# An encoder layer with split fp32 products: where the high parts of eleven weight chunks are made

## The chip, the cores and the metric

The kernel runs on one core of a Trainium2 chip. The metric is the time on the device in microseconds (us), lower is better. All times of the trace are us from the start of the span of one profiled execution. The engines are TensorE (PE; PEld is its weight load), VectorE (DVE), ScalarE (ACT), GpSimd (POOL) and SyncE (SP). Each of SP, ACT and POOL can issue transfers; 16 DMA engines carry them all out.

## The reference

One encoder layer on 256 tokens of width 1024, followed by a final RMSNorm.

```python
h = rmsnorm(x, g1);  proj = h @ w_in + b_in          # q | k | v | lru-x | lru-gate | merge gates
attn = block_attention(rope(norm(q)), rope(norm(k)), v)
xc   = depthwise_conv(xr);  lru = rglru(xc, forward) + rglru(xc, backward)
rec  = lru * gelu(yr)
x    = x + (sigmoid(gA) * (attn @ w_attn_o) + sigmoid(gR) * (rec @ w_lru_o)) @ w_out
x    = x + moe_ffn(rmsnorm(x, g2))                   # 32 experts, top 4, clamped SwiGLU
out  = rmsnorm(x, final_g)
```

## The kernel before

**Two halves.** The first, to about 234 us, is the token mixer. It reads its weights as 15 chunks `pre[0..14]` of 128 rows by 4096 fp32 numbers, 2 MiB each (chunk 3 is half as wide). The second is the mixture of experts: 32 experts of 12 MiB each, in pieces of 2 MiB, stream through a ring of eight slots.

**Split products.** In the first half a product of fp32 operands is made of three passes over rounded operands (type fp32r): high by high, high by low, low by high (`product`, L1033). So every weight chunk `whole(c)` is turned into a high part `high(c)`, which is the chunk rounded to fp32r, and a low part `low(c) = whole(c) - high(c)`, which takes the place of the chunk itself. The high part lies in the slot beside the chunk. Three such pairs of slots turn in a ring, so chunk c can be loaded only when chunk c-3 has been used (`CONSUMED[c - 3]`, L245).

**Who makes the parts.** SP loads the whole chunk (L310). ACT rounds it to the high part in two instructions of 2048 columns (`split_high`, L386). For chunks 5 and 9 (`CAST_V`) DVE does it in one instruction (L631, recorded at L624). DVE subtracts (`split_low`, recorded at L627). PE waits for the low part (`chunk_in`, L1030), except for chunk 0: `first_groups` (L1065) starts with the high part and takes the low part as its last pass.

**What sets the order.** Each engine's program is written out by hand, and semaphores join them. At the start SP issues, without a wait: x in two loads, chunks 0 and 1, two rows of constants sent to all partitions, chunk 2, the tables and the first gate weights. ACT issues the unit squares `sq` and the small constants `cst` (L363, L364). DVE waits for `cst` at L619, works out the norm of x (L594, L600), and turns PE's transposes into `hT_hi` (two halves, L609 and L624) and `hT_lo`. PE's first product, L1078, waits for both ACT instructions on chunk 0 (`split_hi` 2) and for the first half of `hT_hi`. Later places named below: the gates of the recurrence (PE L1092, read by ACT at L419, the second set after the sum L767 on DVE), the rotary part on DVE (L713 to L734) and its transposes on PE (L1120), and the entry of the branches on PE at L1190, which waits for `rec_split` (DVE) and for `group_read` 32 (ACT L406). GpSimd does nothing but four constant fills.

Of the kernel before, what the change touches and what calls it, by code (L numbers as in the profile page):

```python
# [40 lines left out]
PAIRS = 3  # L41
PRE = 15
# [13 lines left out]
def encoder_layer(nc, x, consts, squares, rows, pre, w_lru, w_gu, w_down, b_down, out):  # L56
# [5 lines left out]
    with ctx:  # L62
# [3 lines left out]
        def sem(name):  # L66
            return ctx.enter_context(nc.semaphore(name))
# [113 lines left out]
        extra_full = [sem(f"extra_full{i}") for i in range(2)]  # L181
        lruw_in = sem("lru_weights_in")
        split_hi, split_lo = sem("chunk_high"), sem("chunk_low")
        h_hi, h_lo, rec_split, attn_split = (sem(n) for n in ("h_high", "h_low", "rec_split", "attn_split"))
        chunk_used = [sem(f"chunk_used{j}") for j in range(PER)]
        gu_done, dn_done = chunk_used[3], chunk_used[5]
# [29 lines left out]
        block = ctx.enter_context(nc.Block())  # L216
# [24 lines left out]
        def slot(s):  # L241
# [3 lines left out]
        CONSUMED = ([(group_done, 4), (group_done, 8), (qkv_done, T), (qkv_done, 2 * T)]  # L245
                    + [(group_done, 12 + 4 * i) for i in range(6)])

        IN_CHUNK, Q_CHUNK, BR_CHUNK, MIX_CHUNK = [0, 1, 4, 5, 6, 7, 8, 9], 2, [10, 11, 13], [12, 14]
        CAST_V = (5, 9)

        def casts_before(c):
            return 2 * sum(b not in CAST_V for b in range(c))

        WIDTH = [KD * 2 * KVW if c == Q_CHUNK + 1 else CH for c in range(PRE)]

# [2 lines left out]
        def low(c):  # L258
            return ring_r[PLACE[c]][:, 0:WIDTH[c]]

        def high(c):
            return (late_r if PLACE[c] == LOWS else ring_r[PLACE[c] + 1])[:, 0:WIDTH[c]]

        def whole(c):
            return ring[PLACE[c]][:, 0:WIDTH[c]]

        def landed(c):
            return slot_full[PLACE[c]], 16 * PLACE[:c + 1].count(PLACE[c])
# [93 lines left out]
        def _(act):  # L362
# [15 lines left out]
            def split_high(c, parts=range(2)):  # L378

                act.wait_ge(*landed(c))  # L380
                if c == 13:
                    act.wait_ge(lru_unit, 3)
                    act.wait_ge(pv_ps, NQ)
                w = WIDTH[c] // 2
                for i in parts:
                    nc.scalar.activation(high(c)[:, i * w:(i + 1) * w], whole(c)[:, i * w:(i + 1) * w],  # L386
                                         ACT.Copy).then_inc(split_hi, 1)
# [69 lines left out]
                sum_squares(hn, x_sb, t)  # L457
            root(1, slice(0, T))
            split_high(0)
            split_high(1)  # L460

            act.wait_ge(lam_e, 1)
            nc.scalar.activation(lam_t[1], lam_t[0], ACT.Exp, scale=-1.0).then_inc(lam_e, 1)
            for i in range(4):
                group(i)
            split_high(Q_CHUNK)
            for i in range(4, 8):
                group(i)
                if i == 5:
                    split_high(Q_CHUNK + 1)  # L470
            split_high(4)
            lru_gates(0, range(4))
            act.wait_ge(qk_inv, 1)
            nc.scalar.activation(qk_rstd, qk_rstd, ACT.Sqrt).then_inc(qk_rs, 1)
            split_high(6)
            for i in range(8, 14):
                group(i)
                if i % 2 == 1:
# [5 lines left out]
            act.wait_ge(group_read, 16)  # L484
            gelu_all = gelu[:, :, :].rearrange("p k n -> p (k n)")
            nc.scalar.activation(gelu_all, gelu_all, ACT.Gelu_apprx_tanh).then_inc(gelu_ok, 1)
            split_high(7)
            for i in range(16, 32):
                if 17 <= i < 21:
                    lru_gates(1, [i - 17])  # L490
                s = i - 18
                if 0 <= s - 2 < NQ:
                    h = s - 2
                    act.wait_ge(pT_ps, h + 1)
                    nc.scalar.activation(probT[:, h % 2, :, :].rearrange("p a n -> p (a n)"), ps[:, 2, :],
                                         ACT.Copy).then_inc(pT_ok, 1)
                if 0 <= s < NQ:
                    act.wait_ge(max_ok, s + 1)
                    for t in range(T):
                        b = (s % 2) * T + t  # L500
                        nc.scalar.activation(prob[:, s % 2, t, :], ps[:, s % 2, t * TOK:(t + 1) * TOK], ACT.Exp,
                                             bias=neg_max[:, b:b + 1], scale=HD ** -0.5,
                                             accum_out=exp_sum[:, b:b + 1]).then_inc(exp_ok, 1)
                if i % 2 == 1:
                    group(i - 1)
                    group(i)
                if 20 <= i < 23:
                    lru_decay(1, i - 20)
                if i == 24:
                    lru_root(1)  # L510
                if i in (18, 19):
                    split_high(8, [i - 18])
                if i in (26, 27):
                    split_high(10, [i - 26])
                if i == 30:
                    split_high(11)
            load_sqrt_table(2)
            for c in range(12, PRE):
                split_high(c)
# [55 lines left out]
            for t in range(T):  # L575
# [3 lines left out]
                                     accum_out=ssum[:, t:t + 1]).then_inc(sq_sum, 1)  # L579
                root(4 + t, slice(t, t + 1))  # L580

        @block.vector
        def _(dve):
            steps = [0]

            def link(ins):

                steps[0] += 1
                ins.then_inc(v_step, 1)
                dve.wait_ge(v_step, steps[0])  # L590
# [32 lines left out]
            def high_part(dst, whole):  # L623
                return nc.vector.tensor_copy(dst, whole)  # L624

            def low_part(dst, whole, hi):
                return nc.vector.tensor_tensor(dst, whole, hi.bitcast(f32), ALU.subtract)  # L627

            def split_high(c):
                dve.wait_ge(*landed(c))  # L630
                link(high_part(high(c), whole(c)))  # L631

            def split_low(c):

                if c not in CAST_V:
                    dve.wait_ge(split_hi, casts_before(c) + 2)
                low_part(low(c), whole(c), high(c)).then_inc(split_lo, 1)

            lam = cst[:, C_LAM:C_LAM + 16]
# [28 lines left out]
            for c in range(KD):  # L668
# [4 lines left out]
                b = cst[:, C_CB + c:C_CB + c + 1]  # L673
# [31 lines left out]
            link(nc.vector.tensor_reduce(qk_rstd, w1.rearrange("p (g d) -> p g d", d=HD), AX.X, ALU.add))  # L705
            link(nc.vector.tensor_scalar(qk_rstd, qk_rstd, 1.0 / HD, EPS, ALU.mult, ALU.add))
            nc.vector.reciprocal(qk_rstd, qk_rstd).then_inc(qk_inv, 1)
            split_high(5)
            split_low(5)
            dve.wait_ge(qk_rs, 1)  # L710
            for t in range(T):
# [100 lines left out]
            for s in range(NQ + 3):  # L812
                if 1 <= s <= NQ:
                    head_norm(s - 1)
                if s < NQ:
                    head_max(s)
                if s >= 4 and s % 2 == 0:
                    pair_attn((s - 4) // 2)

                if s == 0:  # L820
                    split_low(7)
                if s == 2:
                    split_low(8)
                if s == 3:
                    lru_input(1)
                if s == 5:
                    lru_square(1)
                if s == 6:
                    split_high(9)
                    split_low(9)  # L830
                if s == 7:
                    lru_scaled(1)
                if s == 8:
                    lru_scan(1)
                    split_low(10)
                if s == 9:
                    lru_sum(1)
                    recurrent_branch()
                if s == 10:
                    recurrent_split()  # L840
# [647 lines left out]
```

## Time and profile before

| | us |
|---|---|
| median of three runs | 1166.57 |
| the three runs | 1162.07, 1167.43, 1166.57 |
| span of the profiled execution | 1161.2 |
| PE busy | 1081.6 |
| ACT busy | 234.2 |
| DVE busy | 382.9 |
| GpSimd busy | 0.2 |

Of the profiled execution the span is what is given; the median of the runs, which are timed from outside, is 5.4 us above it and the lowest 0.9 us. Read the first half and the second apart: in the first PE is busy nearly without a gap and the DMA engines have room, in the second the DMA engines are full and PE waits in small pieces.

### The profile page before, as it was taken

The numbers are of one execution on the slowest core, as the hardware profiler recorded it, in microseconds if no ns is written. First come the engines' busy times: TensorE is split into PE (matmuls) and PEld (weight loads), VectorE is DVE, ScalarE is ACT, GpSimd is POOL, SyncE is SP. The second block draws the span as 40 slices with busy tenths as digits, with TensorE's granted clock in tenths as the row PEclk, the third lists the DMA queues.
The fourth block names the chain that finished last, engine by engine and source line by source line (L and its number), as shares of the span: only waits on it lengthen the run. The fifth ranks groups of instructions, "written<-read, shape, count | busy, mean of one in ns | idle before, by whom it ended". The sixth has DMA issues, their size and how long they took to land.

```text
span 1161.2 us, 13145 instructions
## 1 busy us (share of the span) xinstructions
PE 1081.6 (93%) x5391; PEld 502.8 (43%) x5391; DVE 382.9 (33%) x671; ACT 234.2 (20%) x371; POOL 0.2 (0%) x4
## 2 busy tenths in 40 slices
PE   5998999989999999999998989898989898989997
PEld 5998789823333333333333323332333233323332
DVE  6996798532322222222121212121211212121122
ACT  5388843100111111111111111111110101010112
POOL 0000000000000000000000000000000000000000
PEclk9999999989999999999999999999999999999999
DMA  8543146998999999999999999999999999999996
GB/s 351 186 171 145 73 160 278 418 400 333 429 397 425 431 425 429 428 428 429 428 429 428 430 428 427 430 428 428 430 428 428 429 428 430 428 427 429 429 428 248
DMA packets 32618, 439.89 MB, mean 379 GB/s; under 512 B 3760, under 2 KB 3888, under 8 KB 5712
## 3 DMA queue, kind: packets, MB, share of 16 engines
q1 hardware_dynamic: 32112, 438.53, 89.9%
q10 hardware_dynamic: 480, 0.99, 0.2%
q8 instruction: 19, 0.31, 0.1%
q14 instruction: 7, 0.06, 0.0%
HBM read 438.46 MB, written 1.05 MB: 378 GB/s over the span
## 4 chain that ended last, share of the span: by engine, by line
PE 61%; DMA 33%; DVE 4%; ACT 1%; issue 1%; SPq 0%; DVEq 0%
DMA slot<-in_w_gu_dram 27%; PE ps L1333 25%; PE ps L1037 12%; PE ps L1342 10%; DMA slot<-in_w_down_dram 6%; PE ps L1305 4%; PE ps L1286 3%; PE ps L1300 1%; PE ps L1387 1%; DVE slot_r L627 1%; PE ps L1092 1%; PE ps L1135 1%; PE ps L1264 1%; PE ps L1156 1%; PE ps L1365 0%
## 5 line engine op out<-in xcount | busy, mean ns | idle before, releaser
L1333 PE MATMUL ps<-slot,lru 128*64 128x512 f32 x880 | 198.9, 595 | 21.0 <-DMA slot<-in_w_gu_dram 20.7
L1342 PE MATMUL ps<-slot,lru 128*64 128x512 f32 x896 | 203.3, 596 | 14.8 <-DMA slot<-in_w_down_dram 14.3
L1333 PE MATMUL ps<-slot,qT 128*64 128x512 f32 x880 | 202.1, 601 | 14.4 <-DMA slot<-in_w_gu_dram 12.9
L1333 PEld LDWEIGHTS ps<-slot,lru 128*64 128x64 f32 x880 | 62.7, 137 | 147.6 <-issue 113.5
L1333 PEld LDWEIGHTS ps<-slot,qT 128*64 128x64 f32 x880 | 62.5, 137 | 147.1 <-issue 134.9
L1342 PEld LDWEIGHTS ps<-slot,lru 128*64 128x64 f32 x896 | 62.3, 137 | 135.4 <-issue 117.1
L558 ACT ACTIVATE lru<-ps 128x512 f32<-128x512 f32 x32 | 19.1, 598 | 419.7 <-PE ps L1333 419.7
L993 DVE TENSOR_TENSOR lru<-ps,cst 128x1024 f32<-128x1024 f32 x32 | 39.2, 1225 | 141.5 <-PE ps L1387 141.5
L970 DVE TENSOR_SCALAR lru<-sq,x_sb,small 128x64 f32<-128x64 f32 x66 | 17.7, 312 | 188.1 <-PE ps L1286 188.1
L1037 PE MATMUL ps<-wide_r,slot_r 128*128 128x256 f32 x492 | 66.2, 286 | 0.2 <-DVE slot_r L627 0.2
L1305 PE MATMUL ps<-lru 128*128 128x512 f32 x136 | 63.9, 593 | 0.9 <-DVE lru L1017 0.9
L1286 PE MATMUL ps<-hn,lru 128*64 128x512 f32 x264 | 63.7, 600 | 0.9 <-DVE lru L907 0.9
L987 DVE COPY lru<-ps 128x512 f32<-128x512 f32 x32 | 22.1, 692 | 127.6 <-PE ps L1333 127.6
L1037 PEld LDWEIGHTS ps<-wide_r,slot_r 128*128 128x128 f32 x492 | 61.3, 191 | 4.6 <-issue 4.1
L560 ACT ACTIVATE lru<-lru 128x512 f32<-128x512 f32 x32 | 20.2, 632 | 198.3 <-DVE lru L997 198.3
L627 DVE TENSOR_TENSOR slot_r<-slot,slot_r 128x4096 fp32r<-128x4096 f32 (+1 forms) x14 | 59.7, 4268 | 0.3 <-ACT slot_r L386 0.2
L544 ACT ACTIVATE qT<-ps 128x512 f32<-128x512 f32 x33 | 19.7, 598 | 160.7 <-PE ps L1286 160.7
L937 DVE TENSOR_TENSOR qT<-ps,cst 128x512 f32<-128x512 f32 x16 | 11.1, 692 | 116.6 <-PE ps L1300 116.6
L386 ACT ACTIVATE slot_r<-slot 128x2048 fp32r<-128x2048 f32 (+1 forms) x24 | 43.1, 1838 | 22.1 <-DMA slot<-in_pre_dram 22.1
L551 ACT ACTIVATE lru<-ps 64x512 f32<-64x512 f32 x63 | 37.3, 592 | 39.4 <-PE ps L1342 38.7
L1387 PEld LDWEIGHTS ps<-sq,lru 128*128 128x128 f32 x256 | 30.9, 193 | 26.8 <-issue 25.2
L937 DVE TENSOR_TENSOR lru<-ps,cst 128x512 f32<-128x512 f32 x17 | 11.8, 692 | 89.5 <-PE ps L1300 89.5
(212 smaller groups left out, 905.1 us busy)
## 6 DMA issues: line engine op xcount, KB each, us to landing
slot<-in_w_gu_dram SPq DMA_DIRECT2D x110, 2048.0 KB, 34.9
slot<-in_w_down_dram SPq DMA_DIRECT2D x55, 2048.0 KB, 33.2
wide<-in_w_gu_dram SPq DMA_DIRECT2D x15, 2048.0 KB, 34.8
slot<-in_pre_dram SPq DMA_DIRECT2D x14, 2048.0 KB, 8.3
wide<-in_w_down_dram SPq DMA_DIRECT2D x8, 2048.0 KB, 35.3
slot<-in_w_lru_dram SPq DMA_DIRECT2D x2, 1024.0 KB, 13.3
wide<-in_w_gu_dram SPq DMA_DIRECT2D x2, 1024.0 KB, 14.8
late<-in_w_gu_dram SPq DMA_DIRECT2D x1, 2048.0 KB, 16.8
```

The costliest lines, as they stand in the source:

```text
L386: nc.scalar.activation(high(c)[:, i * w:(i + 1) * w], whole(c)[:, i * w:(i + 1) * w], ACT.Copy).then_inc(split_hi, 1)
L551: nc.scalar.activation(pair_out[i // 2 % 2][rs, side * BANK:(side + 1) * BANK], ps[64 * side:64 * side + 64, bank, :], ACT.Copy).then_inc( ...
L627: return nc.vector.tensor_tensor(dst, whole, hi.bitcast(f32), ALU.subtract)
L937: nc.vector.tensor_tensor(xgT[i % 2].rearrange("p (h k) n -> p k h n", h=2), ps[:, 7, :].rearrange("p (k h n) -> p k h n", k=KD // 2, h=2) ...
L987: nc.vector.tensor_copy(gu_sb[:, 0:BANK], ps[:, 4, :]).then_inc(gu_v, 1)
L993: nc.vector.tensor_tensor(gub.rearrange("p (j n) -> p j n", j=16), ps[:, 4:6, :].rearrange("p b (j n) -> p (b j) n", n=CAP), bias.unsqueez ...
L1037: ins = nc.tensor.matmul(dst, st[a], mv[b], start=start and q == 0 and k == 0, stop=stop and q == 2 and k == len(sides) - 1)
L1286: ins = nc.tensor.matmul(ps[64 * h:64 * h + 64, 7, :], sel_next[:, t, :], x2[:, t, h * BANK:(h + 1) * BANK], start=(t == 0), stop=(t == T ...
L1305: return nc.tensor.matmul(ps[:, n, :], sgT[pair][:, n // 2, :], pair_out[pair][:, (n % 2) * BANK:(n % 2 + 1) * BANK], start=False, stop=last)
L1333: ins = nc.tensor.matmul(ps[64 * side:64 * side + 64, 4 + b, :], xgT[i % 2][:, k, :], rows[r][:, o:o + BANK], start=(k == 0), stop=(k == K ...
L1342: ins = nc.tensor.matmul(ps[64 * side:64 * side + 64, bank, :], actT[(i - 1) % 2][:, k, :], w[:, r, side * BANK:(side + 1) * BANK], start= ...
L1387: ins = nc.tensor.transpose(ps[:, 4 + j // 4, j % 4 * P:(j % 4 + 1) * P], gu_sb[:, j::KD], ident)
```

## The change

The high parts of chunks 1 to 11 are no longer made from the chunk in SBUF. GpSimd's queue issues a second load of the same rows of `pre`, whose destination is the fp32r tensor, so that the transfer rounds. ACT keeps the casts of chunks 0, 12, 13 and 14 (`CAST_A`). DVE's two casts go. Before its subtraction DVE now waits for both loads of the chunk (`landed`, `high_landed`) where it waited for ACT's cast. GpSimd's loads follow the same rule of release as SP's (`CONSUMED[c - PAIRS]`); those of chunks 1 and 2 wait for nothing.

```diff
-        CAST_V = (5, 9)
+        CAST_A = (0, 12, 13, 14)
...
+        def high_landed(c):
+            return high_in[c % PAIRS], 16 * sum(b % PAIRS == c % PAIRS for b in range(c + 1) if b not in CAST_A)
...
             split_high(0)
-            split_high(1)
...
+        @block.gpsimd
+        def _(pool):
+            for c in range(PRE):
+                if c in CAST_A:
+                    continue
+                if c >= PAIRS:
+                    pool.wait_ge(*CONSUMED[c - PAIRS])
+                pool.dma_start(high(c), pre[c, :, 0:WIDTH[c]]).then_inc(high_in[c % PAIRS], 16)
...
-            def split_high(c):
-                dve.wait_ge(*landed(c))
-                link(high_part(high(c), whole(c)))
-
             def split_low(c):
 
-                if c not in CAST_V:
+                if c in CAST_A:
                     dve.wait_ge(split_hi, casts_before(c) + 2)
+                else:
+                    dve.wait_ge(*landed(c))
+                    dve.wait_ge(*high_landed(c))
                 low_part(low(c), whole(c), high(c)).then_inc(split_lo, 1)
```

The calls `split_high(1)`, `(2)`, `(3)`, `(4)`, `(6)`, `(7)`, `(8)`, `(10)` and `(11)` on ACT and `split_high(5)` and `(9)` on DVE are taken out where they stood; nothing else moves.

GpSimd's program, which before the change ends with its constant fills:

```order
L1478 ISA
L1478 MEMSET const-float32-0.0 128x1
L1478 MEMSET const-float32-1.0 128x1
L1478 MEMSET const-bfloat16-1.0 128x1
L1478 MEMSET const-uint8-127 128x1
```

and the same with the change (`slot_r` are the high parts, `in_pre_dram` the chunks in memory):

```order
L1475 MEMSET const-uint8-127 128x1
L573 UNCONDITIONAL_BRANCH [waits barrier_Pool_Activation_PE_DVE_SP_gather]
L580 DMA slot_r<-in_pre_dram 128x4096 x2
L580 DMA slot_r<-in_pre_dram 128x2048 [waits group_done]
L580 DMA slot_r<-in_pre_dram 128x4096 [waits group_done]
L580 DMA slot_r<-in_pre_dram 128x4096 [waits qkv_done] x2
L580 DMA slot_r<-in_pre_dram 128x4096 [waits group_done] x5
```

Eleven loads have come in, the first two of them at the very start.

ScalarE's program from the root of the first norm on, before:

```order
L371 ACTIVATE small<-small 128x2 [waits var_inv]
L386 ACTIVATE slot_r<-slot 128x2048 [waits slot_full0]
L386 ACTIVATE slot_r<-slot 128x2048
L386 ACTIVATE slot_r<-slot 128x2048 [waits slot_full2]
L386 ACTIVATE slot_r<-slot 128x2048
L463 ACT_TABLE_LOAD
L463 ACTIVATE small<-small 128x16 [waits lam_exp]
L397 ACTIVATE xr_flat<-ps,cst 128x256 [waits half_bias_ok,margins,group_done]
L397 ACTIVATE xr_flat<-ps,cst 128x256 [waits group_done] x3
L386 ACTIVATE slot_r<-slot 128x2048 [waits slot_full4]
L386 ACTIVATE slot_r<-slot 128x2048
```

and now:

```order
L375 ACTIVATE small<-small 128x2 [waits var_inv]
L390 ACTIVATE slot_r<-slot 128x2048 [waits slot_full0]
L390 ACTIVATE slot_r<-slot 128x2048
L466 ACT_TABLE_LOAD
L466 ACTIVATE small<-small 128x16 [waits lam_exp]
L401 ACTIVATE xr_flat<-ps,cst 128x256 [waits half_bias_ok,margins,group_done]
L401 ACTIVATE xr_flat<-ps,cst 128x256 [waits group_done] x7
```

Chunk 0 (`slot_full0`) is still rounded here; chunks 1 and 2 are not.

VectorE's program at chunk 5, between the norm of q and k and the rotary part, before:

```order
L705 TENSOR_REDUCE small<-xr_flat 128x20 [waits v_step]
L706 TENSOR_SCALAR small<-small 128x20 [waits v_step]
L707 RECIPROCAL small<-small 128x20 [waits v_step]
L624 CAST slot_r<-slot 128x4096 [waits slot_full4]
L627 TENSOR_TENSOR slot_r<-slot,slot_r 128x4096 [waits v_step]
L713 TENSOR_TENSOR xr_flat<-late,small 128x640 [waits qk_rs]
```

and now:

```order
L704 TENSOR_REDUCE small<-xr_flat 128x20 [waits v_step]
L705 TENSOR_SCALAR small<-small 128x20 [waits v_step]
L706 RECIPROCAL small<-small 128x20 [waits v_step]
L627 TENSOR_TENSOR slot_r<-slot,slot_r 128x4096 [waits chunk_high_in2,slot_full4]
L711 TENSOR_TENSOR xr_flat<-late,small 128x640 [waits qk_rs]
```

The cast is gone, and the subtraction waits for two loads, with the rotary part queued behind it.

## Rows read from the trace of the kernel before

**Rows 1.** The page: busy share of the DMA engines, 40 slices of 29 us.

```profile
DMA  8543146998999999999999999999999999999996
```

**Rows 2.** Stretches: start:end and length, busy us (x instructions) of PE, PEld, DVE, ACT, POOL, clock, DMA share, GB/s.

```profile
27.00:64.00 37.00, 36.27 (x228) 32.42 (x228) 35.21 (x69) 17.33 (x26) 0.00 (x0) 1.00 0.55 199
64.00:104.00 40.00, 36.84 (x294) 35.94 (x293) 32.98 (x35) 34.76 (x50) 0.00 (x0) 1.00 0.36 132
104.00:168.00 64.00, 62.88 (x425) 53.04 (x424) 52.26 (x66) 48.01 (x92) 0.00 (x0) 1.00 0.28 103
...
240.00:290.00 50.00, 47.34 (x197) 17.09 (x198) 10.98 (x34) 4.31 (x6) 0.00 (x0) 0.96 0.90 355
...
330.00:1161.00 831.00, 772.78 (x3504) 274.90 (x3500) 175.47 (x338) 91.36 (x153) 0.00 (x0) 1.00 0.99 421
```

**Rows 3.** Who waited for whom, 0 to 240 us: us in total, times, longest.

```profile
PE ps L1092 <- ACT lru L419: 3.6, 4, 3.2
...
PE ps L1037 <- DVE wide_r L627: 1.1, 1, 1.1
...
PE ps L1078 <- ACT slot_r L386: 0.7, 1, 0.7
...
PE ps L1037 <- DVE slot_r L627: 0.2, 1, 0.2
```

**Rows 4.** Timeline of the start: start, us, engine, line, operation [idle before it, releaser].

```profile
6.56 1.06 ACT L366 ACTIVATE hn<-x_sb 128x1024 f32<-128x1024 f32 x1 [3.38 <-DMA x_sb<-in_x_dram]
...
7.84 0.17 DVE L619 TENSOR_SCALAR cst<-cst 128x16 f32<-128x16 f32 x1 [6.88 <-DMA cst<-in_consts_dram]
...
11.52 3.71 ACT L386 ACTIVATE slot_r<-slot 128x2048 fp32r<-128x2048 f32 x2 [2.13 <-DMA slot<-in_pre_dram]
...
15.29 4.10 PE L1078 MATMUL ps<-wide_r,slot_r 128*128 128x256 f32 x32 [0.65 <-ACT slot_r L386]
15.61 0.69 DVE L624 CAST wide_r<-slot 128x1024 fp32r<-128x1024 f32 x1
...
18.55 8.76 DVE L627 TENSOR_TENSOR slot_r<-slot,slot_r 128x4096 fp32r<-128x4096 f32 x2
...
27.36 2.17 PE L1037 MATMUL ps<-wide_r,slot_r 128*128 128x256 f32 x16 [0.25 <-DVE slot_r L627]
```

**Rows 5.** Stretches of 2 us near the start, columns as in rows 2.

```profile
2.00:4.00 2.00, 0.00 (x0) 0.00 (x0) 0.00 (x0) 1.17 (x2) 0.00 (x0) 1.00 0.81 288
...
10.00:12.00 2.00, 1.02 (x5) 1.05 (x6) 0.84 (x2) 0.48 (x1) 0.00 (x0) 1.00 1.00 426
```

**Rows 6.** DMA issues by line: count, KB each, median us from issue to landing.

```profile
slot<-in_pre_dram SPq DMA_DIRECT2D x14, 2048.0 KB, 8.3
...
x_sb<-in_x_dram SPq DMA_DIRECT2D x2, 512.0 KB, 4.8
...
cst<-in_consts_dram ACTq DMA_DIRECT2D x1, 68.0 KB, 6.6
```

**Rows 7.** The page's groups: ACT's casts (busy, mean ns | idle before), and one of DVE's from the timeline.

```profile
L386 ACT ACTIVATE slot_r<-slot 128x2048 fp32r<-128x2048 f32 (+1 forms) x24 | 43.1, 1838 | 22.1 <-DMA slot<-in_pre_dram 22.1
...
63.64 2.23 DVE L624 CAST slot_r<-slot 128x4096 fp32r<-128x4096 f32 x1
```

**Rows 8.** Timeline, three later places of the first half.

```profile
79.25 0.50 DVE L734 COPY pbuf<-late 128x256 f32<-128x256 f32 x2
...
81.00 1.04 PE L1120 MATMUL ps<-sq,late 128*128 128x128 f32 x8
...
88.27 0.84 ACT L400 ACTIVATE late<-ps,cst 128x256 f32<-128x256 f32 x2 [0.85 <-PE ps L1037]
...
166.73 0.84 ACT L406 ACTIVATE xr_flat<-ps,cst 128x256 f32<-128x256 f32 x2 [1.31 <-PE ps L1037]
...
167.81 2.17 PE L1037 MATMUL ps<-lru_r,slot_r 128*128 128x256 f32 x16 [1.12 <-DVE wide_r L627]
```

**Rows 9.** SP's queue, 0 to 400 us: what the issue of the ring's loads waited for.

```profile
SPq L293 <- PE ps L1333: 113.5, 22, 17.9
```

More of the change, by code:

```diff
@@ L183, in encoder_layer @@
         split_hi, split_lo = sem("chunk_high"), sem("chunk_low")
+        high_in = [sem(f"chunk_high_in{i}") for i in range(PAIRS)]
         h_hi, h_lo, rec_split, attn_split = (sem(n) for n in ("h_high", "h_low", "rec_split", "attn_split"))
@@ L248, in encoder_layer @@
         IN_CHUNK, Q_CHUNK, BR_CHUNK, MIX_CHUNK = [0, 1, 4, 5, 6, 7, 8, 9], 2, [10, 11, 13], [12, 14]
-        CAST_V = (5, 9)
+        CAST_A = (0, 12, 13, 14)
         def casts_before(c):
-            return 2 * sum(b not in CAST_V for b in range(c))
+            return 2 * sum(b in CAST_A for b in range(c))
+        def high_landed(c):
+            return high_in[c % PAIRS], 16 * sum(b % PAIRS == c % PAIRS for b in range(c + 1) if b not in CAST_A)
         WIDTH = [KD * 2 * KVW if c == Q_CHUNK + 1 else CH for c in range(PRE)]
@@ L465, in _ @@
                 group(i)
-            split_high(Q_CHUNK)
             for i in range(4, 8):
                 group(i)
-                if i == 5:
-                    split_high(Q_CHUNK + 1)
-            split_high(4)
             lru_gates(0, range(4))
@@ L474, in _ @@
             nc.scalar.activation(qk_rstd, qk_rstd, ACT.Sqrt).then_inc(qk_rs, 1)
-            split_high(6)
             for i in range(8, 14):
@@ L486, in _ @@
             nc.scalar.activation(gelu_all, gelu_all, ACT.Gelu_apprx_tanh).then_inc(gelu_ok, 1)
-            split_high(7)
             for i in range(16, 32):
@@ L510, in _ @@
                     lru_root(1)
[L511 to L516, printed above, removed]
             load_sqrt_table(2)
@@ L707, in _ @@
             nc.vector.reciprocal(qk_rstd, qk_rstd).then_inc(qk_inv, 1)
-            split_high(5)
             split_low(5)
@@ L828, in _ @@
                 if s == 6:
-                    split_high(9)
                     split_low(9)
```

## The prediction, made before the result was known

> **What bounds the kernel now.** I read the busy tenths of the page first, then the stretches, then who waited for whom, then the timeline at the places that these name. The tenths show the DMA engines with room only between about 30 and 175 us [rows 1]. The stretches say why: from 27 to 168 us PE is busy 36.27 of 37, 36.84 of 40 and 62.88 of 64 us, all at a granted clock of 1.00 (the upper level, 2.4 GHz), while the DMA share is 0.55, 0.36 and 0.28 [rows 2]. After 330 us the DMA share is 0.99 at 421 GB/s [rows 2]: the experts are a stream of fixed bytes. SP's loads for the ring wait for PE to free slots [rows 9], and in 240 to 290 us the DMA share is still 0.90 [rows 2], so the stream can't start ahead of PE. Hence the rule of the whole sum: PE's first half sets when the stream runs, and a shift of PE in the first half, either way, arrives at the end one for one.
>
> So the question is what PE waits for in the first half. Between its first product and 240 us, waits that an engine of the casts ended are few [rows 3]: 0.65 us for ACT's cast of chunk 0, 0.25 us for DVE's low part of chunk 1, 1.12 us for the split of the recurrent branch, and 3.6 us for ACT's reads of the recurrence's gates. The rest is the start: PE's products begin at 15.29 us, released by ACT's cast of chunk 0, which ran from 11.52 to 15.23 right after that chunk had landed [rows 4].
>
> **What the change removes.** On ACT, 18 of the casts (26 in all, of which the group in [rows 7] holds 24), at a mean of 1.84 us [rows 7] about 33 us. On DVE two casts, near 2.23 us each [rows 7], 4.5 us. How much of that lies on the path?
> - Chunk 1's low part held PE for 0.25 us [rows 4]. It was DVE's own queue (two subtractions, 8.76 us in a row), not ACT. In the new kernel PE's start moves later than DVE's (below), and this wait goes: -0.25.
> - At 167.81 PE waited 1.12 us for DVE's split. DVE now comes 2.3 us earlier, having lost a cast at chunk 9. But PE also waits there for ACT's last read, which starts when PE's last group ends (at 166.7, row with 1.31 us idle) and ends at 167.57 [rows 8]. So 167.81 becomes about 167.67: -0.15.
> - The largest wait, 3.2 of the 3.6 us before the second set of gates [rows 3], comes down a chain that begins with ACT's read at 88.27, itself released by PE (0.85 us idle) [rows 8], then root, scans and sum. No cast of ACT or DVE lies in it: 0.
> - All other casts lie beside a busy PE. ACT's queue is shorter, which nobody waits for: 0.
> The gain is 0.4 us, and it can't be more than 0.65 + 0.25 + 1.12, about 2 us, even if every wait at a cast went.
>
> **What it adds.** Eleven loads, 10 x 2.10 + 1.05 = 22.0 MB, at 426 GB/s [rows 5] 52 us of all DMA engines. Nine of them, for chunks 3 to 11, start in stretches where the DMA share is 0.28 to 0.55 [rows 2], with PE two chunks away from needing them. The tightest is chunk 5, with both loads released as PE's third chunk is used and chunk 6's close behind: four transfers of 2.10 MB, 20 us at full rate, where one takes 8.3 us to land now [rows 6]. Behind DVE's wait for it stands the rotary part, which ends at 79.75 for a PE that comes at 81.00 [rows 8]: 1.25 us of slack and 2.23 us from the cast that is gone, 3.5 us. With the pairs sharing evenly chunk 5 lands near 63 us, about when DVE is there (63.64): 0.
>
> The two that wait for nothing, chunks 1 and 2 (4.19 MB), are another matter. Up to 11.5 us the DMA engines are what everybody waits for: from 4 us on they run full (426 GB/s at 10 to 12 us) [rows 5], and x, the small constants and chunk 0 are on the path. Whatever GpSimd's stream moves before chunk 0 has landed delays chunk 0 by its bytes / 426 GB/s. How many bytes is that? No row shows GpSimd's queue. The nearest row on sharing is ACT's: its 68 KB of constants took 6.6 us to land, longer than 512 KB of x (4.8) [rows 6], since their small packets took turns with SP's large ones. I take one packet of each queue in turn, and a packet to be a row of the transfer. Then on each DMA engine x is 16 packets of 4 KiB, chunk 0 is 8 of 16 KiB, and GpSimd's stream is 16 of 16 KiB. SP's first bytes move from 2 us on; by 4 us some 0.6 of the 1.4 MB of x, squares and constants are through (288 GB/s for 2 us) [rows 5], so about 9 packets of x are left. If GpSimd's stream is there by then, 9 + 8 = 17 turns come before chunk 0 is complete, and all 16 of GpSimd's packets go ahead of it: **4.19 MB / 426 GB/s = +9.8 us**. From below: a stream that starts after 11.5 us costs 0. From above: a rounding transfer that runs at half rate holds the engines for twice as long, +19.7 us. Between these ends I take 9.8, as GpSimd has nothing else to do at the start and SP's first issue shows that queues open at once.
>
> What is late next: x would land some 7 us later instead of at 6.5, so the norm, the transposes and both halves of `hT_hi` (the second ends at 16.30 now [rows 4]) come at about 23.5. Chunk 0 lands at 21.3 and its cast ends at 25.1: chunk 0 stays the later one, PE starts at 15.29 + 9.8 = 25.1. DVE's low part of chunk 0 then runs 25.1 to 29.5, that of chunk 1 to 33.9, while PE's first groups last 12 us, to 37: covered, chunk 1's 4.4 us and both loads of it too.
>
> From 2 to 4 us DVE is busy 0.00 us [rows 5], so nothing on it could hold back what GpSimd does at the start. The Trainium skill, SBUF — State Buffer, section "Who interferes with whom", has a rule by which it could: while VectorE runs a two-port copy or tensor_scalar, GpSimd can't write its descriptors and its DMA stands still. No row here can show that; with an idle VectorE the delay of chunk 0 stays 9.8 us by the rule as without it, and later it could only stretch loads that have cover.
>
> **Sum.** +9.8 - 0.25 - 0.15 = +9.4 us, made in the profiled execution: a span of 1161.2 + 9.4 = 1170.6. The 5.4 us between that span and the median lie outside both, so 1166.57 + 9.4 = **1176.0 us**, +0.8%.
>
> **Rivals.**
> - A, as summed, 8 to 11 us later at the start: 1174 to 1178. Chance 0.42.
> - B, a smaller share: GpSimd's packets are smaller than a row, say 4 KiB. 17 turns of 16 engines x 4 KiB are 1.1 MB, +2.6 us, less 0.4: 1168.8. A start of the stream only at 6 us, with x through and 8 turns left, gives 2.1 MB, +4.9 - 0.4: 1171.1. 
> - C, not slower: GpSimd's first descriptors come so late that chunk 0 has landed. The mechanism is the same sharing, and its point is 11.5 us: a stream whose first packet comes after that costs nothing, and 0.4 us are won, 1166.2. Against it: 11 us are long for a queue that has nothing ahead of it. Chance 0.13.
> - D, the rounding halves the rate of its transfers: +19.7 - 0.4, 1185.9, and chunk 5's high part, with 3.5 us of slack, may add 1 or 2. For it: rounding is work that a copy doesn't have; no row prices it. Chance 0.16.
> - E, something in the first half gains that I count as covered; bounded by the 2 us above, it would read as no change. Chance 0.05.
>
> **How the numbers follow.** The likeliest is A: 1176.0. The range takes in B, A and D and leaves C and E and the tail of D out: 1168 to 1187. A measurement of this kernel tells about 0.5% (5.8 us) from no change. Slower by more: A, D and the upper edge of B, 0.62. Within: most of B, C and E, 0.32. Faster by more: only what the scatter of the runs could give, 0.06.
>
> **What would show it.** In the profile after: ACT's first cast (chunk 0) near 21 instead of 11.5 us, and PE's first product near 25; x landing near 13; then the same PE stretches as before, shifted by the same amount, with no new wait of DVE for a load that reaches PE; ACT's busy time down 33 us with no wait of PE for ACT gone but at the start. It would be wrong if GpSimd's packets came after 11.5 us or were few before that (then C or B), if the first half became shorter than the shift by more than 2 us (then a cast was on the path that I don't see), or if DVE idled for loads at chunks 4 to 6 (D).

## The result, and the profile after

The changed kernel took 1174.14 us (median of 6 runs, 1168.97 to 1176.82) beside 1163.68 us (6 runs, 1162.07 to 1167.43) for the kernel before: a ratio of 1.008, 95% interval 1.0063 to 1.0097. It is slower, by some 9.3 us by the ratio and by 10.5 by the two medians; forecast were +9.4 us and 1176.0. The profiled execution has a span of 1171.7 us, 10.5 more than that of before.

That agreement is better than the reasoning was. The early stream cost less than I had summed, and in the profiled execution two things that I had not summed cost the rest. First the page: busy time by engine, the DMA tenths in 40 slices, the queues, and the two groups of DMA issues.

```profile
PE 1086.0 (93%) x5391; PEld 506.2 (43%) x5391; DVE 378.9 (32%) x669; ACT 203.7 (17%) x353; POOL 6.2 (1%) x15
...
DMA  9896557998999999999999999999999999999995
...
q0 software_dynamic: 1584, 22.02, 4.5%
...
slot<-in_pre_dram SPq DMA_DIRECT2D x14, 2048.0 KB, 11.4
slot_r<-in_pre_dram POOLq DMA_DIRECT2D x10, 2048.0 KB, 13.5
```

Queue 0 is GpSimd's: 22.02 MB, as counted from the diff. The hollow in the DMA tenths [rows 1] is partly filled. A load for chunk 1 to 14 takes 11.4 us to land in the median, where it took 8.3 [rows 6]. Now the start: timeline, start, us, engine, line, operation, and the idle time before it with its releaser. It answers to [rows 4].

```profile
1.23 1.19 POOL L580 DMA_DIRECT2D slot_r<-in_pre_dram  x2 [0.78 <-POOLq L1475]
...
7.99 1.06 ACT L370 ACTIVATE hn<-x_sb 128x1024 f32<-128x1024 f32 x1 [4.80 <-DMA x_sb<-in_x_dram]
...
10.49 0.17 DVE L619 TENSOR_SCALAR cst<-cst 128x16 f32<-128x16 f32 x1 [9.53 <-DMA cst<-in_consts_dram]
...
17.85 3.71 ACT L390 ACTIVATE slot_r<-slot 128x2048 fp32r<-128x2048 f32 x2 [6.59 <-DMA slot<-in_pre_dram]
...
21.61 5.54 PE L1075 MATMUL ps<-wide_r,slot_r 128*128 128x256 f32 x32 [5.12 <-ACT slot_r L390]
```

GpSimd issues its two loads at 1.23 us. Chunk 0 is there at 17.85 and not at 11.52 (+6.33), and PE's first product starts at 21.61 and not at 15.29 (+6.32). x is late by 1.4 us only. The first 32 products then take 5.54 us where they took 4.10. Who had the DMA engines? The queues in two stretches of 1 us, 4 to 5 and 5 to 6 (queue, kind: packets, MB, share of 16 engines; q1 is SP's, q10 ACT's):

```profile
q1 hardware_dynamic: 94, 0.33, 81.4%
q10 hardware_dynamic: 76, 0.08, 24.8%
...
q0 software_dynamic: 14, 0.23, 57.7%
q1 hardware_dynamic: 45, 0.18, 45.4%
q10 hardware_dynamic: 47, 0.03, 8.2%
```

and in 8 to 10 us, the window asked for as 8:10:

```profile
q1 hardware_dynamic: 27, 0.44, 53.2%
q0 software_dynamic: 26, 0.43, 50.8%
q10 hardware_dynamic: 26, 0.01, 1.7%
```

GpSimd's first packet moves only after 5 us, some 4 us after the issue: one packet of its queue from 5.0 to 5.2 us, seven from 5.2 to 5.4. From 8 to 10 us the three queues take turns packet by packet (27, 26, 26), and SP gets half of the bytes. If a stream that takes half starts at s, what SP had left to move until 11.5 us takes twice as long, so chunk 0 lands at s + 2 x (11.5 - s) = 23 - s. This is an estimate, made after the result. With s = 5.2, as read, it gives 17.8; measured 17.85. It isn't always so close: two kernels below, whose stream starts at 5.5 us (none of its packets before), should land chunk 0 at 17.5 and do at 18.13 and 18.30.

The next place is the hole before the second set of gates. Timeline of PE, of before and then of after:

```profile
101.75 1.97 PE L1092 MATMUL ps<-wide,slot 128*128 128x256 f32 x8 [3.16 <-ACT lru L419]
...
104.70 2.17 PE L1037 MATMUL ps<-wide_r,slot_r 128*128 128x256 f32 x16
...
107.67 0.60 PE L1092 MATMUL ps<-wide,slot 128*128 128x256 f32 x2
```

```profile
108.95 2.51 PE L1089 MATMUL ps<-wide,slot 128*128 128x256 f32 x8 [3.15 <-ACT lru L423]
...
113.39 3.78 PE L1034 MATMUL ps<-wide_r,slot_r 128*128 128x256 f32 x16
...
117.96 0.60 PE L1089 MATMUL ps<-wide,slot 128*128 128x256 f32 x2
```

The same products, 5.92 us before and 9.01 after, are 3.1 us longer, and the stretches show at which clock. Columns as in [rows 2], of after, an undisturbed stretch and this one:

```profile
27.00:64.00 37.00, 37.00 (x264) 34.97 (x263) 34.73 (x64) 3.68 (x9) 2.11 (x4) 1.00 0.85 330
...
110.00:120.00 10.00, 10.00 (x42) 7.90 (x41) 5.89 (x6) 5.09 (x13) 0.53 (x1) 0.66 0.11 23
```

From 27 to 64 us PE is busy all the time at 1.00, with the DMA share up from 0.55 to 0.85: the later loads don't reach it. From 110 to 120 us the granted clock is 0.66, between its upper level (2.4 GHz) and its lower (1.2), just behind a hole of 3.15 us in PE's work. The whole account of the profiled execution:

| PE reaches | before | after | later by |
|---|---|---|---|
| first product | 15.29 | 21.61 | 6.32 |
| second groups | 27.36 | 34.67 | 7.31 |
| transposes of the rotary part | 81.00 | 88.21 | 7.21 |
| second set of gates | 101.75 | 108.95 | 7.20 |
| the set after it | 107.67 | 117.96 | 10.29 |
| recurrent branch | 167.81 | 177.96 | 10.15 |
| first product of the experts | 240.34 | 250.45 | 10.11 |
| span | 1161.2 | 1171.7 | 10.5 |

6.3 us come from the start; 1.0 up to the second groups, where the first 32 products are 1.44 slower and 0.46 are won where the low part of chunk 1 was waited for, 0.25 of it the wait itself; 3.1 go with the lower clock, and -0.14 come at the branch. The 10.11 at the experts become 10.5 by the end. The waits of PE between 0 and 260 us, which answer to [rows 3], show only these two for engines of the casts and the gates:

```profile
PE ps L1075 <- ACT slot_r L390: 5.1, 1, 5.1
...
PE ps L1089 <- ACT lru L423: 3.6, 4, 3.2
```

Not all runs carry the same. The six runs of the changed kernel had mean granted clocks of 0.994, 0.994, 0.993, 0.991, 0.987 and 0.987, at 1168.97, 1169.42, 1173.29, 1175.0, 1176.82 and 1175.33 us. The two at 0.994 lie some 5.5 us over the median of before, near what the start alone costs. The clock doesn't order all runs, though: at 1173.29 it was 0.993.

### The profile page after: what moved, and what is told of

Its sections match the earlier page's. It is cut to its first block, busy times and chain, and to the rows that moved or that the text cites. A ratio compares the mean times of both kernels' runs of the same rounds, so it can differ in the third digit from the quotient of the medians.

```text
span 1171.7 us, 13145 instructions
## 1 busy us (share of the span) xinstructions
PE 1086.0 (93%) x5391; PEld 506.2 (43%) x5391; DVE 378.9 (32%) x669; ACT 203.7 (17%) x353; POOL 6.2 (1%) x15
## 3 DMA queue, kind: packets, MB, share of 16 engines
q0 software_dynamic: 1584, 22.02, 4.5%
## 4 chain that ended last, share of the span: by engine, by line
PE 63%; DMA 34%; DVE 1%; ACT 1%; issue 1%; SPq 0%; DVEq 0%
DMA slot<-in_w_gu_dram 27%; PE ps L1330 25%; PE ps L1034 13%; PE ps L1339 10%; DMA slot<-in_w_down_dram 6%; PE ps L1302 4%; PE ps L1283 3%; DMA slot<-in_pre_dram 1%; PE ps L1075 1%; PE ps L1297 1%; PE ps L1384 1%; PE ps L1089 1%; PE ps L1132 1%; PE ps L1153 1%; PE ps L1261 1%
## 5 line engine op out<-in xcount | busy, mean ns | idle before, releaser
L1384 PE MATMUL ps<-sq,lru 128*128 128x128 f32 x256 | 37.0, 287 | 0.8 <-DVE lru L984 0.8
## 6 DMA issues: line engine op xcount, KB each, us to landing
slot<-in_pre_dram SPq DMA_DIRECT2D x14, 2048.0 KB, 11.4
```

The costliest lines, as they stand in the source:

```text
L1384: ins = nc.tensor.transpose(ps[:, 4 + j // 4, j % 4 * P:(j % 4 + 1) * P], gu_sb[:, j::KD], ident)
```

## The experiments

My theory: packets of a second stream take turns with chunk 0's at the start, everything else in the change is covered, and the stretch of lower clock has a cause of its own. Rivals: the nine later loads or the removed casts matter (E), the rounding is what is expensive (D), the size of packets or the start of the stream decides (B).

**Casts of chunks 1 and 2 back on ScalarE.** The nine later loads stay; the two early ones go.

```
-        CAST_A = (0, 12, 13, 14)
+        CAST_A = (0, 1, 2, 12, 13, 14)
...
             split_high(0)
+            split_high(1)
...
                 group(i)
+            split_high(Q_CHUNK)
```

> The changed kernel, but with the high parts of chunks 1 and 2 made by ScalarE again, so that GpSimd's queue carries only chunks 3 to 11, each released as PE uses a chunk. Theory (the whole loss is the two loads that wait for nothing and go ahead of chunk 0): chunk 0 lands at 11.5 us and PE's first product starts at 15.3 as before, and the time is that of the kernel before to within 2 us, since the nine later loads and the casts that they replace are both hidden. Rival 1 (the later loads cost too, through DMA contention or VectorE's wait at chunk 5): PE's first product at 15.3, yet 3 us or more slower than before. Rival 2 (the casts taken away did cost something): faster than before by over 2 us.

Measured: 1164.38 us (12 runs) beside 1164.97 for before, ratio 1.0002 [0.9991, 1.0014]. The recurrent branch starts after 0.98 us of idle PE, where before had 1.12: the gain of 0.14 is there, and too small for the time to show. Nine loads of 18 MB in place of 14 casts on ScalarE and two on VectorE are together worth nothing here that the interval shows, in either direction; whether a small gain and a small cost cancel wasn't tried. Its profile has one more thing to keep in mind: chunk 0 is there at 11.71, the first product starts at 15.47 after 0.67 us of idle PE, all as before, and yet the first 32 products take 5.70 us and not 4.10.

**Only the two early loads, all other casts as before.**

```
+        BY_LOAD = (1, 2)
...
+        @block.gpsimd
+        def _(pool):
+            for c in BY_LOAD:
+                pool.dma_start(high(c), pre[c, :, 0:WIDTH[c]]).then_inc(high_in[c], 16)
...
```

> The kernel before, with only chunks 1 and 2 rounded by GpSimd's loads at the start; all other casts as before. Theory (early loads): the whole loss of the change: chunk 0 lands near 17.9 us instead of 11.5, PE's first product near 21.6 instead of 15.3, time 7 to 10 us above before. Rival (later loads carry the loss): under 3 us above before.

Measured: 1173.31 us (6 runs), ratio 1.0073 [1.0054, 1.0091]. So the two early loads account for the whole of the loss, within the intervals; with the run above, the early and the later loads have each been tried alone. Its profile shows both extra terms once more (chunk 0 at 18.13, first product at 21.89, 6.33 us for the first 32), and here the clock can be seen in the first products too. Stretches of 20 to 25, 25 to 30 and 110 to 120 us:

```profile
20.00:25.00 5.00, 3.11 (x14) 3.11 (x15) 3.92 (x2) 3.34 (x4) 0.00 (x0) 0.52 1.01 423
25.00:30.00 5.00, 5.00 (x37) 5.00 (x36) 5.00 (x2) 0.00 (x0) 0.00 (x0) 0.80 1.08 449
...
110.00:120.00 10.00, 9.98 (x35) 7.97 (x36) 4.16 (x3) 7.12 (x14) 0.00 (x0) 0.54 0.00 0
```

**Is it the rounding?** The kernel before, with its casts, and GpSimd copies the same 4.19 MB without rounding into a buffer that is idle then. Nobody reads the copies; ScalarE waits for them before it writes the gates there (left out of the cut above; so it is in the next two kernels with copies).

```
+        @block.gpsimd
+        def _(pool):
+            for i in range(2):
+                pool.dma_start(lru[:, i * CH:(i + 1) * CH], pre[1 + i, :, :]).then_inc(idle_in, 16)
```

> As the run with plain copies on ScalarE's queue, but issued by GpSimd. Theory (rounding costs the transfer nothing, the late start belongs to GpSimd's queue): first packets near 5 us, chunk 0 lands near 17.9 us, as with the rounding loads, x at 8.0. Rival (rounding is what starts late or runs at another rate): chunk 0 lands over 1 us away from 17.9, towards 21 if the plain stream starts early.

Measured: 1171.09 us (4 runs), ratio 1.0051 [1.0033, 1.0069]. Chunk 0 lands at 18.30, no earlier than with rounding (17.85; 18.13 in the run above, whose stream starts at 5.5 us as this one's does), and the first product starts at 22.06. The rounding costs a transfer nothing that shows: D falls. The queues of the changed kernel from 8 to 10 us say the same: 0.44 + 0.43 + 0.01 MB in 2 us are 440 GB/s, with the rounding stream as half of it.

**The same copies on ScalarE's queue,** behind the squares and the constants.

```
             act.dma_start(cst[:, 0:C_COS], consts[:, 0:C_COS]).then_inc(cst_in, 16)
+            for i in range(2):
+                act.dma_start(lru[:, i * CH:(i + 1) * CH], pre[1 + i, :, :]).then_inc(idle_in, 16)
```

> The kernel before with all its casts, and 4.19 MB more to load at the start: chunks 1 and 2 once more, as plain copies on ScalarE's queue into space that is idle until the recurrence's gates. If the delay of chunk 0 is the bytes that get in ahead of it in equal turns of the queues, and the 6.3 us of the change (not 9.8) come from GpSimd's stream starting only at 5 us, then here, with the stream there from 2.6 us on, x is held back by several us (first ScalarE instruction on it at 10 us or later instead of 6.6) and chunk 0 lands at 20 to 21.5 us instead of 11.5: 9 to 10 us later, time 9 to 13 us above before. Rival (a queue's share, not its start, made the 6.3): chunk 0 lands near 18 us here too.

Measured: 1169.81 us (5 runs), ratio 1.0042 [1.0026, 1.0058]; chunk 0 at 15.46, first product at 19.22. That missed what I expected (20 to 21.5, +9 to 13 us), and my rival's 18 too. I had taken the issue (1.67 us) for the start. But from 5 to 6 us ACT's queue still moves its small packets, 83 of them with 0.04 MB in all, and so it does until 7.5 us. ACT's queue from 7 to 7.5 and from 7.5 to 8 us, then both queues from 8 to 10 us:

```profile
q10 hardware_dynamic: 16, 0.00, 2.8%
...
q10 hardware_dynamic: 13, 0.15, 69.2%
...
q1 hardware_dynamic: 28, 0.46, 53.5%
q10 hardware_dynamic: 23, 0.38, 43.9%
```

ACT's queue works in order here, and one turn moves one packet, so the squares (256 KB) and the 68 KB of constants, in packets of about 0.5 KB at the end, hold up the 2 MB loads behind them for as long as they need turns. The stream begins at 7.5 us, and 23 - 7.5 is 15.5; measured 15.46. I formed the rule of 23 - s on this miss. It can't hold for a stream that has run out before chunk 0 is there; then all its bytes go ahead, which the next two try.

**A stream that is there at once:** the copies first on ScalarE's queue, the squares and the constants on GpSimd's.

```
-            act.dma_start(sq[:, :, :], squares).then_inc(sq_in, 16)
-            act.dma_start(cst[:, 0:C_COS], consts[:, 0:C_COS]).then_inc(cst_in, 16)
+            for i in range(2):
+                act.dma_start(lru[:, i * CH:(i + 1) * CH], pre[1 + i, :, :]).then_inc(idle_in, 16)
...
+            pool.dma_start(sq[:, :, :], squares).then_inc(sq_in, 16)
+            pool.dma_start(cst[:, 0:C_COS], consts[:, 0:C_COS]).then_inc(cst_in, 16)
```

> The kernel before with all its casts, and 4.19 MB more to load: plain copies of chunks 1 and 2 as the first thing on ScalarE's queue, with the squares and the small constants moved to GpSimd's. It tries the assumption of the prediction as it stood: a stream that is there from about 2.5 us on. Expected by it: x, in packets of 4 KiB that take turns with packets of 16 KiB, lands at 13 to 15 us instead of 6.6, chunk 0 at about 21.3 instead of 11.5, PE's first product near 25, the time 9 to 13 us above before. Rival (the delay never exceeds about 6.5 us): chunk 0 at 18.

Measured: 1174.27 us (4 runs), ratio 1.0082 [1.0063, 1.0100]. Chunk 0 at 21.49, first product at 25.26: the 21.3 and 25.1 of the prediction, now that its premise holds. x lands at 15.99. The queues from 4 to 6 us show the turns at their plainest:

```profile
q10 hardware_dynamic: 36, 0.59, 69.2%
q1 hardware_dynamic: 36, 0.15, 18.3%
q0 software_dynamic: 6, 0.02, 3.0%
```

36 packets each, but 0.59 MB of the stream (rows of 16 KiB) and 0.15 MB of x (rows of 4 KiB). Turns are equal, bytes are not.

**One early load,** the second held until chunk 0 has landed.

```
             for c in range(PRE):
...
+                if c == 2:
+                    pool.wait_ge(*landed(0))
```

> The changed kernel, but only chunk 1's rounding load starts at once; chunk 2's waits until chunk 0 has landed. Theory (bytes ahead of chunk 0): 2.10 MB from 5.2 us on in equal turns, so chunk 0 lands at 11.5 + 2.10/0.428 = 16.4 us instead of 17.9, PE's first product at 20.2 instead of 21.6, the time 1 to 1.5 us under the changed kernel's. Rival (what counts is that the stream is there, not its bytes): 17.9 us as before.

Measured: chunk 0 at 16.45, first product at 20.22, both as expected: 2.10 MB / 426 GB/s = 4.9 us. All of one load is through ahead of chunk 0. 1170.77 us (4 runs), ratio 1.0065 [1.0042, 1.0087], is 6.4 over its own before (1164.34), more than the 4.9 of the start: its runs lie at 1167.49 and 1168.93 with clocks of 0.997 and 0.995, and at 1172.60 and 1174.09 with 0.990.

**Both early loads held until chunk 0 has landed.**

```
+                if c == 1:
+                    pool.wait_ge(*landed(0))
```

> The changed kernel with one wait more: GpSimd issues its first load only when chunk 0 has landed (11.5 us). Theory (equal turns of the queues from the moment the stream starts, some 4 us after the issue): nothing is ahead of chunk 0, PE's first product at 15.3 us; chunk 1's high part lands at 23 to 25 us, its low part ends at 28 to 29.5, and PE's second groups start there instead of at 27.4: the time is 0 to 2.5 us above the kernel before and 6 to 9 below the changed kernel's 1174. Rival (GpSimd's loads slow the kernel in another way than through chunk 0): over 4 us above before.

Measured: 1164.44 us (12 runs), ratio 1.0007 [0.9995, 1.0019]. Issue, first product, low parts and second groups:

```profile
11.84 1.20 POOL L582 DMA_DIRECT2D slot_r<-in_pre_dram  x2 [11.39 <-DMA slot<-in_pre_dram]
...
15.33 4.10 PE L1077 MATMUL ps<-wide_r,slot_r 128*128 128x256 f32 x32 [0.85 <-ACT slot_r L390]
...
18.62 8.79 DVE L629 TENSOR_TENSOR slot_r<-slot,slot_r 128x4096 fp32r<-128x4096 f32 x2
...
27.46 2.17 PE L1036 MATMUL ps<-wide_r,slot_r 128*128 128x256 f32 x16 [0.29 <-DVE slot_r L629]
```

With this one wait the change costs nothing that the interval shows: the 9.3 us are gone, and the wait for the low part of chunk 1 stays at 0.29, though I had allowed 2.5 us for its high part to be late. All eleven rounding loads are still there.

**The clock.** Does the hole in PE's work bring the lower clock on? Three kernels give PE transposes of a constant whose result nobody reads. The first has 24 while it waits for the norm, 20 before its first product and 24 in the hole; the second has those of the hole alone; the third is the kernel before with those of the hole.

```
+            def idle_transposes(bank, o, times):
+                for _ in range(times):
+                    nc.tensor.transpose(ps[:, bank, o:o + P], ident, ident)
...
             for i in range(16, 32):
                 group(i)
+                if i == 18:
+                    idle_transposes(3, 0, 24)
```

The two calls that the first kernel has at the start, `idle_transposes(7, TOK, 24)` and `idle_transposes(7, TOK, 20)`, stand before and behind its transposes of the norm.

> The changed kernel with transposes that nobody reads added on PE where it stands idle: 24 before its first transposes, 20 before its first product, 24 in the gap ahead of the second set of gates (about 105.7 to 109 us). In the changed kernel's profile the 32 first products took 5.54 us instead of 4.10, and at 110 to 120 us the granted clock was 0.66 (1.2 GHz for part of it), which cost PE 3 us; the kernel before showed neither. Theory (PE's idle time before them is what lets the clock stay or fall low): both go, first products 4.1 us for 32, granted clock 1.00 in 110 to 120 us, time 3 to 5 us below the changed kernel's. Rival (the spells have nothing to do with PE's idle time): they stay, or turn up elsewhere, and the time is that of the changed kernel or above.

> The changed kernel with the same 24 idle transposes in the gap ahead of the second set of gates (105.7 to 109 us), nothing at the start. Theory: first product at 21.6 to 22 us, no low clock at 110 to 120 us, time 2 to 4 us under the changed kernel's 1174, that is 1.005 to 1.007 of before. Rival (the gap's spell is chance): 1.008 of before, with spells in the profile or without.

> The kernel before with 24 idle transposes on PE in the gap of 3.2 us ahead of the second set of gates (98.6 to 101.7 us), nothing else. Theory (the spells after that gap, which the run with idle work lost, are part of the scatter of both kernels): no spell of low clock or slow products at 102 to 115 us, and the runs scatter less, median 0 to 2 us below before. Rival (they are chance and not PE's idle time): the same time and scatter as before, or 0.5 us above it where the transposes outlast the gap.

Measured: the changed kernel with all three 1168.63 us (7 runs), 1.0034 [1.0020, 1.0047]; with those of the hole 1169.91 (5 runs), 1.0049 [1.0035, 1.0062]; the kernel before with them 1162.65 (11 runs), 0.9989 [0.9977, 1.0001]. The hole in the second of these:

```profile
106.79 2.78 PE L1094 MATMUL ps<-sq 128*128 128x128 f32 x24
110.10 1.97 PE L1089 MATMUL ps<-wide,slot 128*128 128x256 f32 x8 [0.52 <-ACT lru L423]
...
113.05 2.17 PE L1034 MATMUL ps<-wide_r,slot_r 128*128 128x256 f32 x16
...
110.00:120.00 10.00, 9.90 (x57) 8.18 (x58) 6.66 (x8) 6.96 (x18) 0.53 (x1) 1.00 0.28 92
```

The hole is filled, the clock is 1.00, and the products take 5.92 us again. The five runs scatter over 1.3 us (1169.05 to 1170.36) where the changed kernel's six do over 7.9, and the interval lies just below that of the changed kernel. That speaks for the hole as a part of the cause. It doesn't settle it. The kernel before with the transposes did not get steadier, against what I had expected: its eleven runs lie 5.0 us apart, the 21 of before 3.5, and its interval includes 1. Before, the casts of chunks 1 and 2 back, the one early load and the stream at once have the same hole of 3.15 us and no lower clock behind it in their profiles, while the kernel with both loads held, which is as fast as before, has 0.79 and 0.87 from 100 to 110 us behind its own, and takes 7.56 us for the products that took 5.92. Nor did the transposes at the start help: in the first kernel the first 32 products took 6.76 us, the longest but one of all, and from 22 to 28 us the granted clock was 0.50, the lower level, though PE had been given 44 transposes more before.

**A version that beats both.** The kernel before, with the transposes in the hole and chunk 0 in two halves, so that ScalarE casts the first while the second is on its way.

```
+                if c == 0:
+                    sp.dma_start(whole(c)[:, 0:CH // 2], pre[c, :, 0:CH // 2]).then_inc(half_in, 16)
+                    sp.dma_start(whole(c)[:, CH // 2:], pre[c, :, CH // 2:]).then_inc(slot_full[PLACE[c]], 16)
...
+            act.wait_ge(half_in, 16)
+            split_high(0, [0])
+            split_high(0, [1])
```

> As the run with idle work in the gap of the kernel before, and chunk 0 loaded in two halves, so that ScalarE casts the first while the second is on its way. Theory (PE's start is bound by chunk 0's landing plus 3.7 us of cast): ScalarE's first cast starts near 9.5 us, the second ends near 13.5, PE's first product starts at 14.4 on the first half of hT_hi instead of 15.3, and the time is 0.9 us below the run without halves. Rival: the start stays at 15.3 because the halves land no earlier.

Measured: 1161.89 us (11 runs) beside 1164.4 (21 runs), ratio 0.998 [0.9971, 0.9989]. It beats before by 2.5 us, 0.2%. ScalarE's casts, PE's first products, the low parts and the second groups:

```profile
9.35 1.90 ACT L392 ACTIVATE slot_r<-slot 128x2048 fp32r<-128x2048 f32 x1
...
11.64 1.91 ACT L392 ACTIVATE slot_r<-slot 128x2048 fp32r<-128x2048 f32 x1 [0.39 <-DMA slot<-in_pre_dram]
...
14.59 4.86 PE L1086 MATMUL ps<-wide_r,slot_r 128*128 128x256 f32 x32
...
18.61 8.75 DVE L635 TENSOR_TENSOR slot_r<-slot,slot_r 128x4096 fp32r<-128x4096 f32 x2
...
27.42 0.74 PE L1045 MATMUL ps<-wide_r,slot_r 128*128 128x256 f32 x4 [0.24 <-DVE slot_r L635]
```

PE starts 0.7 us earlier and has lost it all by 27.42: there it waits for VectorE's low part of chunk 1, the second of the two subtractions in a row that start at 18.61, as before at 18.55. Beside the kernel with the transposes alone (1162.65, ratio 0.9989) the intervals overlap, so how the 2.5 us divide between the two edits isn't settled; in this profile the halves gave nothing that lasted.

## Why the prediction was right, and where it wasn't

- **PE bounds the first half, and a shift passes to the end one for one.** Right to within 2 us: 10.29 us after the second gates, 10.11 at the experts, 10.5 in the span. Over all thirteen profiles the rest, from the experts' first product to the end, takes 919.0 to 921.3 us; that of before (920.9) is near the long end, and the one early load, 6.3 us late at the experts, ends 4.4 us late. The two loads alone give 1.0073, all eleven 1.008.
- **The removed casts are covered.** Right. ScalarE's busy time fell by 30.5 us to 203.7 (33 forecast) and VectorE's by 4.0 to 378.9 (4.5); the run with the casts of chunks 1 and 2 back reads 1.0002. The two small gains came as summed, 0.25 (no wait at 34.67) and 0.14 (branch).
- **Nine later loads are hidden.** Right in the time, with less to spare than I wrote. For chunk 5 I had VectorE wait for nothing; it waited 4.59 us for the high part. The timeline of it, and of the end of the rotary part:

```profile
72.54 4.43 DVE L627 TENSOR_TENSOR slot_r<-slot,slot_r 128x4096 fp32r<-128x4096 f32 x1 [4.59 <-DMA slot_r<-in_pre_dram]
...
85.88 0.50 DVE L732 COPY pbuf<-late 128x256 f32<-128x256 f32 x2
...
88.21 1.04 PE L1117 MATMUL ps<-sq,late 128*128 128x128 f32 x8
```

  The rotary part ends at 86.38, PE comes at 88.21. Of the slack of 3.5 us, 1.8 are left.
- **Turns packet by packet, packets as large as a row.** Right: 27, 26 and 26 packets in 2 us, and 0.23 MB in 14 packets, 16 KiB each. B with packets of 4 KiB falls, and D by the copies without rounding.
- **The stream is there by 4 us.** Wrong, and this is the term that was mis-sized: +9.8 was +6.3. I took the start of GpSimd's queue from SP's, which issues at 0.75 us and runs at 288 GB/s from 2 us on [rows 5]. GpSimd's came 4 us after its issue. With it fell "x some 7 us later": 1.4. B had named this very case (a start at 6 us, +4.9) and I gave all of B 0.24. Where the stream is there at once, the sum holds to 0.2 us (21.49 for 21.3), and the time is 9.9 us over its before.
- **The same PE stretches as before, shifted.** Wrong twice, and unforeseen: 1.44 us in the first 32 products and 3.1 us in a stretch of lower clock, in this profile. I had read 1.00 in the clock column of before and taken it for granted after a shift. These two make up for what the start cost less. That the shift brings them on isn't shown: the first also came without a shift (5.70 us with the casts of chunks 1 and 2 back), and the second with PE's start on time (both loads held).
- **The level of 1176.0.** It stood on the three runs of before that there were, 1166.57. With six they read 1163.68, so by the same sum the forecast would be 1173.1.

So the forecast was near by luck as to its size, and for a reason that was only part of mine: in the profiled run start +6.3, the stretch of the first products +1.0, clock +3.1, branch -0.14. The first term alone stays in every profile of these early loads (6.2 to 6.7 us); the lower clock doesn't, which fits the two of six runs that read 1169, whose profiles weren't taken.

What stays open: why the clock was lower behind the same hole in some kernels' runs and not in others, and why the first 32 products take 4.1 to 6.8 us. For the latter the clock column is no full answer; it reads 1.00 from 20 to 30 us in the changed kernel (5.54 us) and with the hole filled (6.82), and 0.52 and 0.80 in the kernel with only the early loads (6.33). The number of products in a stretch of 1 us says more. PE alone, in the first 32 products of the kernel with only the early loads, of the changed kernel, and of before (a product that lies partly in the stretch counts). Columns: stretch and length, PE busy (x products), clock, DMA share, GB/s:

```profile
23.90:24.90 1.00, 1.00 (x7) 0.50 0.93 393
...
22.60:23.60 1.00, 1.00 (x7) 1.00 1.21 508
...
17.30:18.30 1.00, 1.00 (x11) 1.00 1.10 444
```

The changed kernel's first products come as slowly at a column of 1.00 as the others at 0.50, the lower level. So they may have run at that level with the column not showing it; no run here tells that from another cause.

## What to carry to other kernels

A prefetch that waits for nothing is not free at the start of a kernel: it takes turns with the load that everybody waits for, and one wait on that load's arrival gave back all of its cost here. Count what goes ahead in turns and not in bytes (a load with small rows loses most), and read the start of a queue from a row of that queue, not of another. And where a sum fits the total, fit each milestone too; here two errors of opposite sign made it fit.

## What the runs showed of the hardware that I had not expected

- GpSimd's first packet comes some 4 us after its issue, at the start and later: issued at 1.23 us, it moves after 5; issued at 11.84 us in the kernel with both loads held, it moves at 15.5 (no packet of its queue from 13 to 15.5 us, 15 from 15.5 to 16). It does so with rounding and without, and for the small squares and constants too (issued at 1.25 us, none from 4 to 5 us, 6 from 5 to 6). The Trainium skill, DMA: Bandwidth & Descriptors, section "Latency and other measured facts", gives about 1 us for the first byte of such a transfer; no run here shows so little. In the changed kernel VectorE was idle for the 9.53 us before 10.49, so the block by VectorE that the prediction weighed can't be the cause of it there.
- A load that rounds moves as fast as a copy (chunk 0 at 17.85 and 18.13 beside 18.30). The same page's section "Queues, rings and completion order" has each DMA engine go round its queues packet by packet; the 36 to 36 packets above agree.
- ACT's queue kept 2 MB loads behind the squares and 68 KB of constants in small packets until 7.5 us, though the loads were issued at 1.67.
- The lower clock behind a hole of 3.15 us cost 3.1 us in one profile and 1.6 in another; in four there was none behind such a hole, and 24 idle transposes in the hole went with a clock of 1.00 in all four kernels that had them.
